# Runs of expert rows on VectorE reach on to the end of the second latent group's gates; latents come back in two loads, and their transposes stand between the context's scans

## The reference, cut to what matters

```python
h = _rmsnorm(x, norm_g[0]) * (1 + sc1) + sh1
proj = h @ w_in            # u, v, zb, q, k, rv, rg_f, rg_b, gm
y_a = gmlp(gelu(u), gelu(v)); y_b = pool(zb); y_c = retention(q, k, rv, ...)
merged = ga * y_a + gb * y_b + gc * y_c
x = x + gt1 * (merged @ w_out)
h2 = _rmsnorm(x, norm_g[1]) * (1 + sc2) + sh2
# PEER: per token 8 heads x 16 experts out of 16,384, found by two top-16 rankings
act = gelu(einsum('thkd,td->thk', u_tab[expert], h2))
x = x + gt2 * einsum('thk,thkd->td', softmax_weights * act, v_tab[expert])
y = _rmsnorm(x, final_norm_g)
```

## Time and profile before

| | us |
|---|---|
| median of 3 runs | 4693.73 |
| lowest, highest | 4682.78, 4695.0 |
| profiled execution, device time | 4679.32 |
| its span from first to last instruction | 4677.6 |
| TensorE busy | 3785.4 (81%) |
| VectorE busy | 2791.3 (60%) |
| ScalarE busy | 1638.0 |
| GpSimd busy | 1609.5 |
| bytes moved | 1672.71 MB, mean 358 GB/s |

### The profile page before, as it was taken

The page is one execution under the profiler, slowest core; times in us unless marked ns, Lnnn a source line. Parts: engine busy times, 40 slices in busy tenths (PEclk is TensorE's granted clock), DMA queues, the critical chain, the costliest instruction groups (busy, mean ns, idle before and its releaser), DMA issues. The chain is left out here.

```text
span 4677.6 us, 44483 instructions
## 1 busy us (share of the span) xinstructions
PE 3785.4 (81%) x12065; PEld 1581.1 (34%) x12065; DVE 2791.3 (60%) x6341; ACT 1638.0 (35%) x5132; POOL 1609.5 (34%) x1312
## 2 busy tenths in 40 slices
PE   5999799898998869999785897889777566666666
PEld 4645355565644323353321232343222111111110
DVE  1112478576676685754699656545588994544444
ACT  4110254432122343432344433323433453333333
POOL 0000033222222233433343434444344445555554
PEclk8999899999999879999896997999777667666666
DMA  7545688888999989999999999999999999999998
GB/s 266 219 175 192 217 298 325 289 300 337 343 391 382 360 318 400 402 381 386 380 393 357 397 398 358 419 385 403 415 391 393 389 402 406 414 421 415 414 421 355
DMA packets 289339, 1672.71 MB, mean 358 GB/s; under 512 B 29185, under 2 KB 71233, under 8 KB 111297
## 3 DMA queue, kind: packets, MB, share of 16 engines
q0 software_dynamic: 184320, 1342.26, 71.9%
q1 hardware_dynamic: 96608, 304.18, 17.2%
q10 hardware_dynamic: 8160, 23.43, 1.5%
HBM read 1631.98 MB, written 37.78 MB: 357 GB/s over the span
## 5 line engine op out<-in xcount | busy, mean ns | idle before, releaser
L1031 POOL DMA_INDIRECT slots<-in_peer,idxR x1280 | 1603.2, 1253 | 3011.7 <-PE ps L1328 1852.4
L1328 PE MATMUL ps<-slots,lhs 128*64 128x512 f32 x4544 | 1507.4, 778 | 690.9 <-ACT lhs L1083 687.4
L1604 DVE CUSTOM_DVE_ANT_0 slots<-slots,h2R 128x1024 f32<-128x1024 f32 x1280 | 1546.5, 1224 | 753.7 <-issue 683.1
L1312 PE MATMUL ps<-ring,arena 128*128 128x512 f32 (+2 forms) x4300 | 1554.1, 519 | 33.0 <-DMA ring<-in_wq 12.7
L1312 PEld LDWEIGHTS ps<-ring,arena 128*128 128x128 f32 x4300 | 786.2, 195 | 827.1 <-issue 772.3
L1328 PEld LDWEIGHTS ps<-slots,lhs 128*64 128x64 f32 x4544 | 298.0, 160 | 1795.8 <-ACT lhs L1083 1563.7
L1072 ACT ACTIVATE gelus<-dots 128x1 f32<-128x1 f32 x1280 | 256.2, 200 | 1495.9 <-DVE dots L1604 1493.4
L1083 ACT ACTIVATE lhs<-fold,wgts 128x64 f32<-128x64 f32 x1136 | 395.1, 348 | 37.1
L1075 ACT ACTIVATE wgts<-gelus,gsmR 128x1 f32<-128x1 f32 x1280 | 377.0, 295 | 42.2
L1312 PE MATMUL ps<-ring,slots 128*128 128x512 f32 (+1 forms) x704 | 249.1, 515 | 0.6 <-DMA ring<-in_wz 0.6
L1616 DVE SCALAR_TENSOR_TENSOR slots<-slots,wgts 128x1024 f32<-128x1024 f32 x135 | 173.0, 1281 | 76.0 <-ACT wgts L1075 70.3
(11 more groups left out here) (196 smaller groups left out, 2277.7 us busy)
## 6 DMA issues: line engine op xcount, KB each, us to landing
ring<-in_whead SPq DMA_DIRECT2D x24, 2048.0 KB, 11.0
ring<-in_wa SPq DMA_DIRECT2D x24, 2048.0 KB, 11.3
ring<-in_wq SPq DMA_DIRECT2D x16, 2048.0 KB, 17.3
slots<-in_peer,idxR POOLq DMA_INDIRECT x1280, 12.5
ring<-in_wlate SPq DMA_DIRECT2D x16, 1024.0 KB, 7.4
ring<-in_wgc SPq DMA_DIRECT2D x16, 1024.0 KB, 9.7
ring<-in_wgb SPq DMA_DIRECT2D x8, 2048.0 KB, 11.6
ring<-in_wout SPq DMA_DIRECT2D x8, 2048.0 KB, 11.9
```

Of the source, the lines that this page charges most:

```text
L1031: g.indirect_dma_start(out=slot(R), out_offset=None, in_=a["peer"], in_offset=bass.IndirectOffsetOnAxis(ap=idxR[:, p % KEEP, g2, col:col + ...
L1312: done = mm(out, lhsT, rhs, start=n == 0, stop=n == len(pairs) - 1)
L1328: done = mm(ps[j * HALF:(j + 1) * HALF, g2, :], weights, slot(R)[:, D + j * UW:D + (j + 1) * UW], start=start, stop=stop)
L1604: v.tensor_tensor_reduce(out=u, in0=u, in1=h2R[:, g2, :], scale=1.0, scalar=0.0, op0=ALU.mult, op1=ALU.add, accum_out=dots[:, R % LHS:R % ...
```

## The change

The mark `last` moves from the first query of group 1 to the first output projection (`wo`) of group 2. By the table that marks rows 80 to 399: 20 runs in place of 9, 176 rows more. The places of all rows between the front's events stay as they are. Of the transposes only the context's (`ht(0)`) stand ahead of stage 0; the 16 of the latents follow two by two, after each context scan step `sA` and ahead of a `late` event, and each pair waits for its own input only. The second `late` of a head stands ahead of the first `sB`. The latents come back in two loads: the first three of eight column blocks after the first query of group 0 (`lin0`), the other five at `lin`; one semaphore for each four chunks, and `hq` waits for its own four chunks only. ScalarE waits for the stores of `hT` before the first gelu of group 0.

```diff
@@ ht, stage
         for n in range(4):
             ev = self.add("ht", 1, i=p, j=n, pe=1.6, act=0.8)
             self.at["ht", p, n] = ev.t
+            yield
...
                 self.at["q", G_, h, seg] = ev.t
-                self.fill()
+                self.fill(2 * G_)
...
             first(0)
             if G_ == FIRST[0]:
+                self.fill()
                 self.late(2 * h)
             for it in range(1, nch):
                 first(it)
+                if G_ == FIRST[0]:
+                    self.fill()
+                    self.late(2 * h + 1)
                 second(it - 1)
             if G_ == FIRST[0]:
-                self.late(2 * h + 1)
                 self.fold(4 + 2 * h)
@@ queries, make_front
             self.query(k, m)
+            if m == 0:
+                self.add("lin0")
...
-        for p in (0, 1, 2, 3, 4):
-            self.ht(p)
+        for _ in self.ht(0):
+            pass
+        self.filler = (tile for p in range(1, NC // 2) for tile in self.ht(p))
@@ merge
-            if ev.kind == "wq" and ev.g == 1 and last is None:
+            if ev.kind == "wo" and ev.g == 2 and last is None:
                 last = n
@@ SyncE
-                elif k == "lin":
+                elif k == "lin0":
                     sp.wait_ge(s["hT_out"], 16 * (NC - CC))
                     for c in GROUPS[0]:
                         sp.wait_ge(x1_out[c], 16)
                         filled(sp, at["h2c", c])
+                    for c in range(CC, NC):
+                        sp.dma_start(hT[1][:, 0:3, (c - CC) * P:(c - CC + 1) * P], hTd[c][:, 0:3, :]
+                                     ).then_inc(hl_in[(c - CC) // 4], 16)
+                elif k == "lin":
                     filled(sp, last_rank)
                     for c in range(CC, NC):
-                        sp.dma_start(hT[1][:, :, (c - CC) * P:(c - CC + 1) * P], hTd[c]).then_inc(s["hl_in"], 16)
+                        sp.dma_start(hT[1][:, 3:KD, (c - CC) * P:(c - CC + 1) * P], hTd[c][:, 3:KD, :]
+                                     ).then_inc(hl_in[(c - CC) // 4], 16)
@@ ScalarE, TensorE
                 elif k == "v":
+                    if ev.g == ev.i == ev.j == 0:
+                        eng.wait_ge(s["hT_out"], 16 * (NC - CC))
...
-                    pe.wait_ge(s["x_done"], 5)
+                    pe.wait_ge(s["x_done"], ev.i + 1)
...
-                        pe.wait_ge(s["hl_in"], 16 * (NC - CC))
+                        pe.wait_ge(hl_in[ev.j], 2 * 16 * 4)
```

More of the change, by code:

```diff
@@ L768, in build @@
             sm_done state_done zero_done zv_done sq_done ms_done std_done x_done tmp_free gate_done in_free
-            h2_done gm_in hl_in cond_done top_done exp_done sum_inv gsm_done idx_done dot_done w_done row_free sum_done
+            h2_done gm_in cond_done top_done exp_done sum_inv gsm_done idx_done dot_done w_done row_free sum_done
             acc0_free acc1_free gt2_in yx_in y_sum y_sq y_ms y_std y_done y_out
@@ L776, in build @@
         x_in = [sem(f"x_in_{b}") for b in range(5)]
+        hl_in = [sem(f"hl_in_{n}") for n in range(2)]
         x1_out = [sem(f"x1_out_{c}") for c in range(NC)]
```

## The result

The changed kernel is slower by 40 us: median 4728.5 us (4724.1 to 4735.7, 4 runs) against 4688.3 (4678.9 to 4695.0, 4 runs), ratio 1.0085, 95% interval 1.007 to 1.010. The forecast was 4717 us and +23; the time lies in the range, the loss is larger than forecast.

A forecast was written before the change was run, and what follows sets the result against it. VectorE was taken to bound group 1's rankings, TensorE group 2's gates, with transfers close behind. Rows +47, start -14 and loads -10 gave +23 us, 4717 us on the median, range 4684 to 4756.

The forecast's parts named there:

- piece 3: Group 1's rankings and first two thirds of group 2's gates, 123 rows: VectorE-bound at 0.96 busy, 484 us, +58 us.
- Piece 4: Last third of group 2's gates, 39 rows: TensorE lightened, transfers end last, -12 us (-13.5 to 0).
- Piece 1: Second norm of group 1, 6 rows, 1507.5 to 1525.6 us: serial stretch, VectorE's added time costs +4 us.
- piece 2: First queries of group 1, 8 rows, 1525.6 to 1566.7 us: VectorE no bound, half of TensorE's shed work shows, -3 us.
- The start: Ahead of and in the first heads: first head some 11.5 us earlier, moved transposes fill TensorE idle time, -14 us.
- The loads: Latents at `lin`: TensorE's wait falls from 17.7 to 7.6 us with half the chunks needed first, -10 us.
- the rows' part: All newly chained rows, second norm of group 1 through group 2's gates: +47 us, ends +18 and +77.
- three signs of being wrong: VectorE under 0.9 from group 1's first query to mid group 2's gates; stretch not longer; first dot under 10 us earlier.
- A: No change: VectorE gapless in rankings and early gates, transfers at 420 GB/s in the last gates, +2 us, 4696; chance 0.21.
- B: Slower: TensorE bound again in group 2's gates at a low clock, 20 us more, 4737; chance 0.14.
- C: Faster: VectorE's arrears paid in its idle time in the last gates and behind the last run, -10 us; chance 0.12.

The follow-up runs named there:

- one-instruction kernel: Rows 80 to 223 chained as before, start and loads as changed; one extra VectorE instruction ahead of the dots of rows 240 to 287: 4722.1 us, 1.0064.
- the half width: Changed kernel with VectorE's addition for rows from 224 on over 512 of 1024 columns, first row of each run full: 4688.1 us, 0.9999.
- the one run: Rows 80 to 223 chained as before, start and loads as changed, plus rows 224 to 239 chained: 4681.6 us, 0.9978.
- without longer runs: Changed kernel with the mark back at its old place, so rows 80 to 223 chained as before; start and loads as changed: 4671.3 us, 0.9957.

## Why the prediction was right, and where it was off

**Direction and mechanism: right, and shown.** VectorE bound in the rankings, its time added there in full: piece 3, rows 238 to 360, was forecast as 484 us at a VectorE share of 0.96 and took 198.1 + 122.5 + 165.9 = 486.5. VectorE was busy 188.8 + 116.8 + 150.2 = 455.9 us of it, a share of 0.94. That the two agree to 2 us is in part luck: VectorE needed 8.6 us less than the 464.5 I had added up, and its share was 0.94, near the 0.935 already seen, and not the 0.96 I chose. In the rankings the one-instruction kernel shows that VectorE's time alone suffices. Nor is VectorE the only bound in the gates, as the half width showed.

**Piece 4, the last gates: right.** Forecast -12, seen -12.9. The transfers run at 399 GB/s and not 420, and VectorE is busy 0.89.

**Pieces 1 and 2: the step that failed.** Piece 1 was +4 and is +4.4. In piece 2 I took the first queries for a place where a lighter TensorE may win 3 us; it lost 13.6 in the trace, and the one run with rows 224 to 239, forecast at +1, costs 10 us by the medians. I had looked at TensorE's and VectorE's busy time there (VectorE: "no bound") and not at what a chained row waits for: a weight from ScalarE, which stands behind TensorE's tile, which stands behind a weight unit. VectorE stood 21.7 us there, just ahead of the stretch that it bounds, and the unit was some 5 us later too.

**The start: mis-sized.** Forecast -14, measured -7.5 alone. The term counted the transposes ahead of the first head and then more from idle time in the heads. The first part was 9 us; in the heads nothing was left over.

**The loads: right.** Forecast -10, measured -10.8 alone; the loads at the queries cost nothing that can be seen.

In sum the rows' part was forecast at +47 and is +54 alone and +57 on the changed start, by the medians; the start and loads were forecast at -24 and are -18 to -20. So of the 17 us between +40 and +23 some 9 come from pieces 1 and 2 and some 6 from the start.

**The signs.** Two of the three signs of being wrong that I had set came out. The first dot is 8.7 us earlier, where I had 20 to 25 and wanted 10 at least. Most of that was a misreading: before, the first dot stands at 568.9 us and TensorE's wait at `lin` ends only at 575.5, so the loads' 10 us cannot show in it; row 27, behind both, is 19.4 us earlier. The rest is the start. And VectorE is busy 412 of the 465 us from 1510.9 us to the middle of group 2's gates (1976), a share of 0.89, where I had over 0.93 and wanted 0.9: the first queries pull it down (22.3 of 54.7 us), and that is the failed piece 2 again. From the rankings on it is 0.95. The wait for `hT_scratch` (8.3 us), the end of the waits for `lhs` and the shorter last window came as said; the stretch with the first queries, to row 360, is 74 us longer, and I had 40 to 70.

**The rivals.** A (no gap in VectorE): no, its share is 0.94. B (TensorE bound again at a low clock): no. The granted clock did fall, from 1.00 to 0.82 and from 0.99 to 0.81 in the gates, as the Trainium skill, TensorE: Matmul & The Clock Gate, section HAM oscillation, would have it for an array that waits for data again and again. The trace agrees with the rule. But TensorE is busy only 79.1 of 122.5 and 106.9 of 165.9 us there at that clock, so it has room for what the clock costs it, and it isn't the bound. What the clock costs shows in the kernel with one instruction more: in the rankings 344 matmuls are busy 121.3 us at 0.71, where without it 342 are busy 109.1 at 0.79. Whether some of that reaches the total through a tile that another engine waits for, no run separates. C (arrears flow out behind the last run): no; the distance of the two traces is 46 us at row 400 and does not shrink, it grows to 56 at the last row.

## What to carry to other kernels

A mean share of 60% says nothing of the room for more work: put new work on an engine by the windows in which it stands, and add its time to the busy time of that window. Where two in-order engines trade the role of the bound from stage to stage, the same edit costs its full time in one stage and brings at most the transfers' slack in the other. And when an operation moves to another engine, look at what it waits for there: here VectorE took over an addition whose weight comes from ScalarE, and with it every wait that stands ahead in ScalarE's queue, 21 us at one place.

## What the runs showed of the hardware that I had not expected

In the crowded place at group 1's first queries a 2 MB weight transfer needed between 15.2 us (without longer runs) and 24.0 us (with the one run) from issue to the waiting engine's start, where the median landing of the query units is 17.3 us before; and SyncE's three group loads took between 4.0 and 12.4 us to issue in kernels that differ only in which engine adds the rows:

```profile
1505.87 12.42 SPq L937 DMA_DIRECT2D arena<-hT_scratch  x3
...
1521.57 3.79 SPq L849 DMA_DIRECT2D ring<-in_wq  x2
```

These are the changed kernel's lines; the kernel with the one run has the same three loads in 4.0 us, the one without longer runs in 8.6. The unit's time does not go by the chained rows alone: with the two loads alone, where no row is chained at this place, it is 19.9 us. Each is of one execution. What stands behind the differences stays open.
